# Hybrid attention block, one core: values and gates projected first, by tiles of tokens, with norm1's gain multiplied in along the tokens

## Time and profile before

| | us |
|---|---|
| median of 3 runs | 656.25 (655.18 to 657.04) |
| the profiled execution's own time | 656.27 |
| its span | 654.4 |
| PE busy in the span | 640.9 (98%) |
| DVE busy | 460.0 (70%) |
| ACT busy | 355.2 (54%) |
| POOL busy | 246.1 (38%) |

### The profile page before, as it was taken

The page is one execution under the profiler, slowest core; times in us unless marked ns, Lnnn a source line. Parts: engine busy times, 40 slices in busy tenths (PEclk is TensorE's granted clock), DMA queues, the critical chain, the costliest instruction groups (busy, mean ns, idle before and its releaser), DMA issues.

```text
span 654.4 us, 11411 instructions
## 1 busy us (share of the span) xinstructions
PE 640.9 (98%) x4059; PEld 573.6 (88%) x4059; DVE 460.0 (70%) x956; ACT 355.2 (54%) x697; POOL 246.1 (38%) x153
## 2 busy tenths in 40 slices
PE   8999999999999999999999999999999999999996
PEld 7888988888899877888878899999999998888884
DVE  5435437746655787735479998888888898788984
ACT  7546446778664558725332474444444446655653
POOL 4766344585151533463312103434443320121522
PEclk9999999999999999999999999999999999999999
DMA  8989979569995996997399957888787678989913
GB/s 243 273 178 229 262 213 222 123 179 356 262 254 120 232 196 185 203 222 210 109 310 284 252 160 244 249 234 237 231 247 201 201 224 286 329 259 256 293 64 128
DMA packets 116007, 146.58 MB, mean 224 GB/s; under 512 B 5252, under 2 KB 73968, under 8 KB 115952
## 3 DMA queue, kind: packets, MB, share of 16 engines
q1 hardware_dynamic: 96936, 110.49, 53.7%
q0 software_dynamic: 16352, 30.84, 27.2%
q10 hardware_dynamic: 2664, 4.53, 2.0%
HBM read 139.53 MB, written 59.00 MB: 303 GB/s over the span
## 4 chain that ended last, share of the span: by engine, by line
PE 92%; DVE 2%; issue 2%; ACT 1%; POOL 1%; DMA 1%; POOLq 0%; ACTq 0%; DVEq 0%
PE bank L816 9%; PE bank L818 9%; PE bank L817 9%; PE bank L1147 8%; PE bank L1145 8%; PE bank L1146 8%; PE bank L835 7%; PE bank L837 7%; PE bank L836 7%; PE bank L988 6%; PE bank L964 3%; PE bank L948 2%; PE bank L949 2%; PE bank L1027 1%; DMA causal<-in_c_causal_dram 1%
## 5 line engine op out<-in xcount | busy, mean ns | idle before, releaser
L765 POOL TENSOR_TENSOR w_lo<-raw,w_hi 128x1024 fp32r<-128x1024 f32 (+1 forms) x63 | 156.2, 2483 | 227.3 <-ACT w_hi L1188 226.6
L1188 ACT CAST w_hi<-raw 128x1024 fp32r<-128x1024 f32 (+2 forms) x123 | 127.0, 1039 | 117.6 <-PE bank L1147 57.6
L1657 DVE CUSTOM_DVE_ANT_0 bank<-bank,bias 128x128 f32<-128x128 f32 (+3 forms) x96 | 47.6, 497 | 76.4 <-PE bank L949 40.5
L835 PE MATMUL bank<-xT_hi,w_hi 128*128 128x512 f32 x208 | 83.4, 401 | 0.8 <-POOL w_lo L765 0.6
L837 PE MATMUL bank<-xT_hi,w_lo 128*128 128x512 f32 x208 | 81.9, 394 | 0.0
L836 PE MATMUL bank<-xT_lo,w_hi 128*128 128x512 f32 x208 | 81.7, 393 | 0.0
L1814 DVE TENSOR_TENSOR w_lo<-raw,w_hi 128x1024 fp32r<-128x1024 f32 (+1 forms) x61 | 73.6, 1207 | 10.6 <-ACT w_hi L1188 10.4
L1145 PE MATMUL bank<-xs,w_hi 128*128 128x256 f32 x256 | 72.3, 282 | 0.0
L1147 PE MATMUL bank<-xs,w_lo 128*128 128x256 f32 x256 | 72.2, 282 | 0.0
L1146 PE MATMUL bank<-xs,w_hi 128*128 128x256 f32 x256 | 72.2, 282 | 0.0
L786 POOL DMA_DIRECT2D down_sums<-in_w_down_dram x21 | 23.3, 1109 | 109.5 <-DVE w_lo L1814 54.8
(11 more groups left out here) (282 smaller groups left out, 1714.5 us busy)
## 6 DMA issues: line engine op xcount, KB each, us to landing
raw<-mixed_sums SPq DMA_DIRECT2D x32, 512.0 KB, 4.4
raw<-in_w_gate_dram SPq DMA_DIRECT2D x22, 512.0 KB, 4.7
raw<-in_w_in_dram SPq DMA_DIRECT2D x20, 512.0 KB, 6.1
down_sums<-in_w_down_dram POOLq DMA_DIRECT2D x17, 512.0 KB, 8.9
mixed_sums<-in_w_up_dram SPq DMA_DIRECT2D x16, 512.0 KB, 11.2
mixed_sums<-in_w_gate_dram SPq DMA_DIRECT2D x16, 512.0 KB, 8.7
mixed_sums<-mixed_sums POOLq DMA_DIRECT2D x16, 512.0 KB, 12.9
raw<-in_w_up_dram SPq DMA_DIRECT2D x14, 512.0 KB, 4.1
```

What stands on the lines that cost most here:

```text
L765: nc.gpsimd.tensor_tensor(wv_lo(k)[:, 0:n], raw_at(k)[:, 0:n], wv_hi(k)[:, 0:n].bitcast(F32), ALU.subtract).then_inc(s_split, 1)
L835: nc.tensor.matmul(bank[:, :], hi, xT_hi[:, kt, :], start=kt == 0, stop=False)
L1188: nc.scalar.copy(wv_hi(k)[:, 0:n], raw_at(k)[:, 0:n]).then_inc(s_whi, 1)
```

## The change

- The first four jobs are now vg 0, vg 1, q 0, k "ksl", and the first chunks of weights those of values and gates.
- SP loads the first tile of x, the two chunks of values and gates, then the other three tiles of x, then the rest as before.
- norm1 comes as one row (gain_row, 1x1024, a DMA that ACT issues first of its four). PE multiplies a column of ones by it, in two matmuls of 512 columns, so two banks (GAIN) hold norm1 in every partition. DVE multiplies x by 1/rms and by this bank in one instruction for each half row (scalar_tensor_tensor, 128x512, two for each tile of tokens), so mix is normed with the gain in.
- The transposes of a tile of tokens go to two banks (TOKENS, alternating between two pairs), four squares in each. ACT copies each half tile to xT_hi, DVE subtracts to xT_lo. A tile of tokens can so be split before the next one is there.
- PE takes the tiles in turn: transposes of tile t, then the 24 matmuls of values and gates of a tile in three groups of 8 (high by high, low x by high weights, high x by low weights). Tile 1's transposes stand behind all matmuls of tile 0; those of tiles 2 and 3 stand ahead of the last group of the tile before.
- The 5 and 3 warming matmuls between tiles go; 3 new ones stand behind the gain matmuls.
- q 0 and "ksl" run as ordinary jobs behind it. The exponential of the gates waits for two evacuated jobs and not four.
- DVE writes all 1120 columns of chunk 1's high part, and does so ahead of the bias vector and ahead of the first tile's low part.

The diff, without the renamed banks and the semaphores:

```diff
-PROJ_JOBS = [("q", 0), ("k", "ksl"), ("vg", 0), ("vg", 1), ("k", "kw"), ("dk", 0), ("dq", 0), ("q", 1),
+PROJ_JOBS = [("vg", 0), ("vg", 1), ("q", 0), ("k", "ksl"), ("k", "kw"), ("dk", 0), ("dq", 0), ("q", 1),
+        GAIN, TOKENS = ps[4:6], [ps[0:2], ps[6:8]]
 @@ SP
-            for t in range(NT):
-                sp.dma_start(xres[:, t, :], x[0, t * P:(t + 1) * P, :]).then_inc(s_x[t], 16)
+            sp.dma_start(xres[:, 0, :], x[0, 0:P, :]).then_inc(s_x[0], 16)
             for k in range(len(chunks)):
+                if k == 2:
+                    for t in range(1, NT):
+                        sp.dma_start(xres[:, t, :], x[0, t * P:(t + 1) * P, :]).then_inc(s_x[t], 16)
 @@ PE
+            def turn_tokens(t):
+                pe.wait_ge(s_norm, t + 1)
+                for half in range(2):
+                    if t >= 2:
+                        pe.wait_ge(s_tlo, 2 * (t - 2) + half + 1)
+                    for z in range(4):
+                        kt = 4 * half + z
+                        mm = nc.tensor.transpose(TOKENS[t % 2][half][:, z * P:(z + 1) * P], mix[:, t, kt * P:(kt + 1) * P],
+                                                 ident[:, :])
+                    mm.then_inc(s_tp, 1)
+            def token_values(t, low):
+                o = ps[2 + t][:, 0:V_COLS]
+                def one(act_, w, kt, first, last):
+                    c = (kt % 4) * V_COLS
+                    return nc.tensor.matmul(o, act_[:, kt, t * P:(t + 1) * P], w[:, c:c + V_COLS], start=first, stop=last)
+                if low:
+                    for half in range(2):
+                        pe.wait_ge(s_split, half + 1)
+                        for kt in range(4 * half, 4 * half + 4):
+                            mm = one(xT_hi, wv_lo(half), kt, False, kt == KT - 1)
+                    if t % 2:
+                        mm.then_inc(s_job, 1)
+                    return
+                for half in range(2):
+                    pe.wait_ge(s_thi, 2 * t + half + 1)
+                    high_done(pe, half)
+                    for kt in range(4 * half, 4 * half + 4):
+                        one(xT_hi, wv_hi(half), kt, kt == 0, False)
+                for half in range(2):
+                    pe.wait_ge(s_tlo, 2 * t + half + 1)
+                    for kt in range(4 * half, 4 * half + 4):
+                        one(xT_lo, wv_hi(half), kt, False, False)
             keep_warm(WARM)
+            pe.wait_ge(s_gain, 16)
+            for half in range(2):
+                mm = nc.tensor.matmul(GAIN[half][:, :], ones[0:1, :], gain_row[0:1, 512 * half:512 * half + 512],
+                                      start=True, stop=True)
+            mm.then_inc(s_gain_p, 1)
+            keep_warm(WARM_GAIN)
+            pe.wait_ge(s_ident, 16)
+            turn_tokens(0)
             pe.wait_ge(s_btab, 16 * 3)
-            nc.tensor.matmul(ps[6][0:NHEADS, 0:384], relb[:, :], choice[:, :], start=True, stop=True).then_inc(s_bvec_p, 1)
+            nc.tensor.matmul(ps[3][0:NHEADS, 0:384], relb[:, :], choice[:, :], start=True, stop=True).then_inc(s_bvec_p, 1)
+            token_values(0, False)
+            token_values(0, True)
+            pe.wait_ge(s_rows, 16 * 6)
+            nc.tensor.transpose(ps[2][:, 384:384 + N_ROWS], rows[0:N_ROWS, :], ident[0:N_ROWS, 0:N_ROWS]).then_inc(s_cols_t, 1)
+            turn_tokens(1)
             pe.wait_ge(s_bvec, 1)
+            token_values(1, False)
+            turn_tokens(2)
+            token_values(1, True)
+            pe.wait_ge(s_norm, NT)
+            token_values(2, False)
+            turn_tokens(3)
+            token_values(2, True)
+            token_values(3, False)
+            token_values(3, True)
 @@ ACT
+            act.dma_start(gain_row[:, :], norm1).then_inc(s_gain, 16)
+            def tokens_hi(t):
+                for half in range(2):
+                    act.wait_ge(s_tp, 2 * t + half + 1)
+                    nc.scalar.copy(xT_hi[:, 4 * half:4 * half + 4, t * P:(t + 1) * P],
+                                   TOKENS[t % 2][half][:, :].rearrange("p (k n) -> p k n", k=4)).then_inc(s_thi, 1)
+            token_norm(0)
             weights_hi(0)
+            tokens_hi(0)
+            token_norm(1)
+            token_norm(2)
+            tokens_hi(1)
+            token_norm(3)
+            tokens_hi(2)
+            weights_hi(2)
+            tokens_hi(3)
+            weights_hi(3)
             act.wait_ge(s_cols, 1)
+            act.wait_ge(s_evac, 2)
+            nc.scalar.activation(gates[:, :, :], gates[:, :, :], ACT.Exp, scale=-1.0).then_inc(s_gexp, 1)
             weights_hi(4)
+            weights_hi(5)
             load_bias(0)
             load_bias(1)
+            for j in (2, 3):
+                for u in range(2):
+                    evac_hi(j, u)
             weights_hi(6)
             weights_hi(7)
 @@ DVE
+            def normal_tokens(t):
                 invert(20 + t, 21 + t)
+                if t == 0:
+                    dve.wait_ge(s_gain_p, 1)
+                for half in range(2):
+                    part_ = slice(512 * half, 512 * half + 512)
+                    ins = nc.vector.scalar_tensor_tensor(out=mix[:, t, part_], in0=xres[:, t, part_], scalar=stat[:, 52 + t:53 + t],
+                                                         in1=GAIN[half][:, :], op0=ALU.mult, op1=ALU.mult)
+                ins.then_inc(s_norm, 1)
+            normal_tokens(0)
+            raw_landed(dve, 1)
+            nc.vector.tensor_copy(wv_hi(1)[:, 0:chunk_cols(1)], raw[:, 1, 0:chunk_cols(1)]).then_inc(s_whi1, 1)
+            dve.wait_ge(s_bvec_p, 1)
+            nc.vector.tensor_tensor(bias_vec[:, :], ps[3][0:NHEADS, 0:384], causal[:, :], ALU.add).then_inc(s_bvec, 1)
+            tokens_lo(0)
+            normal_tokens(1)
+            normal_tokens(2)
+            tokens_lo(1)
+            normal_tokens(3)
+            tokens_lo(2)
+            tokens_lo(3)
```

More of the change, by code:

```diff
@@ L51 @@
 WARM = 12
-WARM_GAP = (5, 3, 0)
+WARM_GAIN = 3
 RAW_SLOTS = 3
@@ L101 @@
                2, 0, 0, 1, 0, 1, 1, 0, 4, 0, 2, 1, 4, 0, 4, 0, 2, 1, 4)
[L102 to L105, removed]
 PIECES = {"ht": 1, "hc": 1, "mt": 1, "og": 4, "od": 4}
@@ L432, in hymba_block @@
                 lam_in = sb("lam_in", [P, 4, HD], F32, begin)
-                sb("under_k_diff", [P, 2560], F32, begin)
+                gain_row = sb("gain_row", [1, D], F32, begin)
+                sb("under_k_diff", [P, 2560 - D], F32, begin)
                 blk_f = sb("blk_f", [P, 2, 16 * GROUPS * NC], F32, begin)
@@ L477, in hymba_block @@
         s_root, s_inv, s_norm = sem("s_root"), sem("s_inv"), sem("s_norm")
+        s_gain, s_gain_p = sem("s_gain"), sem("s_gain_p")
         s_tp, s_thi, s_tlo = sem("s_tp"), sem("s_thi"), sem("s_tlo")
@@ L993, in _ @@
             pe.wait_ge(s_ones, 1)
             keep_warm(WARM)
-            pe.wait_ge(s_btab, 16 * 3)
-            nc.tensor.matmul(ps[6][0:NHEADS, 0:384], relb[:, :], choice[:, :], start=True, stop=True).then_inc(s_bvec_p, 1)
[L997 to L1012, removed]
-            pe.wait_ge(s_bvec, 1)
[L1014 to L1034, removed]
+            pe.wait_ge(s_gain, 16)
+            for half in range(2):
+                mm = nc.tensor.matmul(GAIN[half][:, :], ones[0:1, :], gain_row[0:1, 512 * half:512 * half + 512],
+                                      start=True, stop=True)
@@ L1310, in _, with token_norm @@
             nc.scalar.activation(stat[:, 63:64], stat[:, 62:63], ACT.Sqrt)
-            for t in range(NT):
+            def token_norm(t):
                 act.wait_ge(s_x[t], 16)
@@ L1317, in _ @@
                 root(20 + t, 21 + t, D)
-            weights_hi(0)
-            act.wait_ge(s_cols, 1)
[L1320 to L1325, removed]
+            def tokens_hi(t):
[4 more added lines that the diff above has]
+            token_norm(0)
+            weights_hi(0)
+            tokens_hi(0)
[7 more added lines that the diff above has]
+            weights_hi(3)
+            act.wait_ge(s_cols, 1)
+            act.wait_ge(s_evac, 2)
+            nc.scalar.activation(gates[:, :, :], gates[:, :, :], ACT.Exp, scale=-1.0).then_inc(s_gexp, 1)
             weights_hi(4)
+            weights_hi(5)
             load_bias(0)
             load_bias(1)
[L1329 to L1333, removed]
+            for j in (2, 3):
+                for u in range(2):
+                    evac_hi(j, u)
             weights_hi(6)
@@ L1740, in _ @@
-            dve.wait_ge(s_cols, 1)
[L1741 to L1745, removed]
+                if t == 0:
[4 more added lines that the diff above has]
+                                                         in1=GAIN[half][:, :], op0=ALU.mult, op1=ALU.mult)
@@ new lines, in normal_tokens, with tokens_lo @@
+                ins.then_inc(s_norm, 1)
+            def tokens_lo(t):
+                for half in range(2):
+                    dve.wait_ge(s_thi, 2 * t + half + 1)
```

(10 more changed lines are left out.)

## The result

The changed kernel takes **661.47 us** (median of 6, 660.65 to 665.35), the kernel before 656.17 (6 runs on the same chip): a ratio of **1.0082**, 95% interval 1.006 to 1.0103. That is 5.3 us slower. Forecast were 657.0 and "within 0.3%" as the likeliest, with 659.3 as the upper end of the range. Three executions that ran far slower as a whole (two of the kernel before, one of experiment 6's) are in no median or ratio here.

What follows compares the result with a forecast made beforehand. PE was taken as the bound, busy 640.9 of 654.4 us. Later stream start 2.0, transposes 1.9, minus matmuls 3.1 and spacing 0.25, plus waits 0.1, gave +0.65, taken as +0.7: 657.0 us, range 655.2 to 659.3.

Steps and rivals of the forecast that it cites:

- Tile 0: First tile's chain: PE transposes 8.95 to 9.9, bias matmul to 10.65, last group of matmuls ending at 14.45.
- PE slows in the gaps: Rival: without warming in the gaps, tile 0's work runs at the early slow pace, adding 2.7 us (659.7); chance 0.05.
- mix of tile 0 at 8.85: DVE's first normed tile, behind gain matmuls from 5.5 to 7.35, ready at 8.85 against 7.06 before.
- the milestone: Start of job "kw" on PE, forecast at 38.3 against 37.6, +0.7 us; the end was to move equally.
- a wait of 1 us on DVE for the gain: Sign of being right: DVE has 1/rms at 6.27 and waits 1.1 us for the gain matmuls.
- Two instructions for mix, 1.4 us: DVE's two half-row instructions replace one of 0.75, costing 0.65 us more for each of four tiles.
- DVE's cast, 0.75: DVE's cast of chunk 1, 1120 columns, takes 0.75 us from its landing at 8.9, to 9.65.
- Chunk 1 late: Rival: DVE waits for chunk 1; past 10.1 each microsecond delays the milestone, 2.0 at 12.1 (659.0); chance 0.20.
- until the semaphore: A 0.8 us term added to chunk 1's load time in forecasting its landing at 8.9.
- Dense from the first matmul of tile 1 on: From 16.05 PE works nearly without waits, 22.3 us in all, up to the start of "kw" at 38.3.
- Behind the milestone nothing: After "kw" starts nothing adds cost: casts have 1.4 us of slack, SP's copies shifting about 1 us cost nothing.
- moves by over 1 us: Sign of being wrong: PE's idle time between 43 and 300 us changes by more than 1 us.

Runs made afterwards that it cites:

- experiment 6: The kernel before plus 8 matmuls on all 128 rows behind the 12 warming ones, as the control: 657.90 us, ratio 1.0029.
- experiment 5: The kernel before plus 8 one-row matmuls of 128 columns behind the 12 warming ones: 660.45 us, ratio 1.0058.
- experiment 2: The changed kernel with the gain matmuls on all 128 rows (127 of zeros, cleared by DVE) and not one: 657.89 us, ratio 1.0024.
- Experiment 4: The kernel before without the 5 and 3 warming matmuls between the tiles of tokens: 656.17 us, ratio 0.9993.
- experiments 7 and 8: 7: experiment 2 with clearing shared by DVE and POOL, norm1's load issued earlier, 1.0031; 8: the same, bias matmul ahead of the first transposes, 1.003.
- experiments 1 and 3: 1: the changed kernel with seven warming matmuls behind the gain, not three, 659.48 us; 3: the same with chunk 1's cast on ACT, not DVE, 658.51 us.

## Why the prediction was wrong, point by point

**The step that failed** is "Tile 0", together with the rival that should have held it. Tile 0's transposes, bias matmul and 24 matmuls were costed at the full clock: 0.95, 0.75 and, waits included, 3.8 us. They took 1.87, 1.38 and 4.96, which is 2.7 us more. The rival "PE slows in the gaps" had the right price (2.7 us) but the wrong cause, gaps without warming, and so a chance of 0.05. I had costed the gain matmuls by their columns and never asked what they are to the clock; I looked for stretches without work, and in experiment 5 the clock fell without one. Experiments 2 and 5 show it: behind one-row matmuls the clock fell, whether PE was otherwise busy (5) or not, and with all rows used it did not. Between the changed kernel and experiment 2 lie 0.58% or 3.8 us. The two profiles account for 2.8 of them by the clock; the rest may be the longer low stretches of the other executions, which is not shown. Experiment 4 shows that the warming which the change removed was worth nothing, as forecast.

**mix of tile 0 at 8.85** came at 10.3, and this is the second term that was too small: 1.5 us. With the 2.7 it makes up the 4.2 by which the milestone came later than forecast (42.5 for 38.3). The gain matmuls took 2.2 and not 1.8. And the warming ended at 6.6 and not 5.5: the first 24 passes take 4.38 us in the execution of the earlier trace rows and 5.49 in others, in the unchanged warming of experiment 4 too. Before, this end was hidden, as PE waited for the bias tables until 6.92; the change hangs its first step on it. I had read the 5.5 of one execution as a fixed time. The sign to look for, a wait of 1 us on DVE for the gain, was 2.5. The same term is the likeliest reason why experiment 2, with the clock kept, stands at 1.0024, 1.6 us, where +0.7 was forecast. There mix ended at 9.9, 1.05 late (norm1 landed at 6.33, and the gain matmuls took 2.0), and from then on the dense stream started as far behind as forecast: 7.1 us after mix against 7.2.

**Two instructions for mix, 1.4 us:** 1.41 in every profile. Right, and with it the doubled rate lost. **DVE's cast, 0.75:** wrong. It took 2.44, with POOL's subtraction from 9.52 to 12.07; its end lay 0.59 behind POOL's end. In the changed kernel it cost nothing (DVE then waited 1.1 us for the bias matmul; the forecast had this wait at 1.2, right, but from two ends that were both wrong). Nor did PE wait for it in experiment 2's chain. It is the next bound once mix comes earlier (experiments 7 and 8). The rows of the changed kernel:

```profile
9.52 2.55 POOL L768 TENSOR_TENSOR w_lo<-raw,w_hi 128x1120 fp32r<-128x1120 f32 x1 [4.43 <-ACT w_hi L1214]
10.22 2.44 DVE L1792 CAST w_hi<-raw 128x1120 fp32r<-128x1120 f32 x1
```

The Trainium skill (SBUF — State Buffer, Who interferes with whom) says that a cast or a tensor_scalar of DVE in its two-port mode and an instruction of POOL lock each other out for a whole instruction. Seven measured ends behind POOL's, 0.54 to 0.61 us, agree with it: five casts (the changed kernel, experiments 1, 2, 7 and 8) and two normed tiles (5 and 6). The page bore on an instruction that the prediction moved next to POOL's work, and I did not weigh it.

**Chunk 1 late.** It landed by 10.2, when DVE starts the cast without a wait, near the limit of 10.1, and the rival did not decide. The forecast had it at 8.9; the 0.8 us "until the semaphore" in that sum stands on no row. **Dense from the first matmul of tile 1 on, 11.3 us to the end of values:** predicted 16.05 to 27.3, measured 20.16 to 31.45. Right in length. **Behind the milestone nothing:** in the medians this holds within what the runs tell, +4.9 at the milestone against +5.3. In the profiled execution it does not. PE's idle time from the milestone to 300 us is 7.3 us for 4.3, and "moves by over 1 us" was named as a sign of being wrong. What I had costed at nothing was the shift of SP's issues in a stretch with DMA share 0.94. The weight chunk that ACT waited 6.1 us for came through that queue. That the new order brings such waits about is likely from the seven profiles against four, but no experiment isolates it.

## What to carry to other kernels

Matmuls on one row of the array are busy time in every view, and yet the clock fell behind 2 us of them: ahead of a stream that matters, pad them to all rows with zeros, or keep them away. (Only one row and all 128 were tried.) When a step is put at the very front, ask whether the time that it starts at was hidden slack before, and how much it varies. A DVE instruction of the fast two-port kind that is moved next to a POOL instruction can cost POOL's remaining time on top of its own: 2.44 us here for a cast of 0.73. And when the order of loads changes, look for waits at a DMA far behind the place of the change too.

## What the runs showed of the hardware that was not expected

- Four passes of 512 columns (changed kernel) or sixteen of 128 (experiment 5) on one row of the array were followed by a granted clock of 0.50, for 6.8 and 3.4 us; the same passes on 128 rows, mostly zeros in experiment 2 and ones in 6, were not. With four more full matmuls behind the one-row ones, the profiled executions of experiments 1 and 3 kept 1.00.
- The same first 24 passes of warming took 4.38 to 5.49 us in different profiled executions, 5.49 in six of eleven, with the granted clock shown as 1.00 throughout: the column shows no difference between an execution in which they were quick and one in which they were slow.
- DVE's cast of 128x1120 took 0.73 with POOL idle, and 1.20 to 2.50 beside it.
